# Attention stage of a YOCO decoder step: projections by token half in two accumulators, o by K half and token half, attention pieces between single K steps

## The reference

```python
def _shared_kv(x, pos, ln_kv, w_kv, k_norm):
    kv = _rms(x, ln_kv) @ w_kv
    ...
    k = _rope(_rms(k, k_norm), pos)
    return k, v

def _sink_attend(q, k, v, mask, sink):
    s = jnp.einsum('...qhgd,...khd->...hgqk', q.astype(jnp.float32), k.astype(jnp.float32)) * (HEAD_DIM ** -0.5)
    s = jnp.where(mask, s, NEG_INF)
    sk = sink.astype(jnp.float32)[:, :, None, None]
    m = jnp.maximum(jnp.max(s, axis=-1, keepdims=True), sk)
    p = jnp.exp(s - m)
    denom = jnp.sum(p, axis=-1, keepdims=True) + jnp.exp(sk - m)
    o = jnp.einsum('...hgqk,...khd->...qhgd', p / denom, v.astype(jnp.float32))

def _window_layer(x, pos, kk, vv, mask, ln, w_q, q_norm, sink, w_o, banded):
    q = (_rms(x, ln) @ w_q).reshape(B, L, N_HEADS, HEAD_DIM)
    q = _rope(_rms(q, q_norm), pos)
    ...
    return o.reshape(B, L, N_HEADS * HEAD_DIM) @ w_o
```

## Time and profile before

| what | value |
|---|---|
| median of three runs | 1665.57 us (1665.43 to 1666.39) |
| the profiled execution: its own time, its span | 1669.15 us, 1667.4 us |
| PE, PEld busy | 1586.8 us (95%), 1469.3 us (88%); 11246 instructions each |
| DVE, ACT, POOL busy | 841.2 us (50%), 510.7 us (31%), 145.3 us (9%) |
| share of the chain that ended last | PE 81%, DVE 9%, ACT 3%, DMA 3%, issue 2% |
| mean granted TensorE clock | 0.972 of full speed |

### The profile page before, as it was taken

The page is one execution under the profiler, slowest core; times in us unless marked ns, Lnnn a source line. Parts: engine busy times, 40 slices in busy tenths (PEclk is TensorE's granted clock), DMA queues, the critical chain, the costliest instruction groups (busy, mean ns, idle before and its releaser), DMA issues.

```text
span 1667.4 us, 27494 instructions
## 1 busy us (share of the span) xinstructions
PE 1586.8 (95%) x11246; PEld 1469.3 (88%) x11246; DVE 841.2 (50%) x1105; ACT 510.7 (31%) x778; POOL 145.3 (9%) x129
## 2 busy tenths in 40 slices
PE   7999999999999899999999999887789999999998
PEld 7688878968987799999999999865679999999997
DVE  6557438536734774434333485664546343443343
ACT  4243144224315332212222243244323221222221
POOL 0000001001000250000000040222132000000001
PEclk9999999999999999999999999885999999999999
DMA  6246217214423442222322232310012222222223
GB/s 229 82 156 212 86 57 253 90 65 167 154 73 104 139 144 87 89 88 77 99 88 89 76 101 86 99 43 14 26 39 78 100 87 91 76 101 77 97 79 104
DMA packets 51314, 166.80 MB, mean 100 GB/s; under 512 B 5920, under 2 KB 6256, under 8 KB 51200
## 3 DMA queue, kind: packets, MB, share of 16 engines
q1 hardware_dynamic: 43808, 137.35, 25.8%
q0 software_dynamic: 6704, 25.99, 4.3%
q10 hardware_dynamic: 720, 2.26, 0.3%
HBM read 141.36 MB, written 23.46 MB: 99 GB/s over the span
## 4 chain that ended last, share of the span: by engine, by line
PE 81%; DVE 9%; ACT 3%; DMA 3%; issue 2%; POOL 1%; DVEq 0%; SPq 0%; ACTq 0%; POOLq 0%
PE ps L422 63%; PE ps L436 8%; PE ps L948 2%; PE ps L942 2%; DVE arena L1384 2%; DVE w_lo L410 1%; PE ps L1192 1%; PE ps L930 1%; DVE x L1384 1%; DMA arena<-in_state 1%; DMA out_st_s<-arena 1%; PE ps L1171 1%; DVE arena L1724 1%; DMA w_raw<-in_w 1%; PE ps L1179 1%
## 5 line engine op out<-in xcount | busy, mean ns | idle before, releaser
L422 PE MATMUL ps<-xg_hi,w_hi 128*128 128x272 f32 x1728 | 363.9, 292 | 15.3 <-DVE xg_lo L1390 8.3
L422 PE MATMUL ps<-xg_hi,w_lo 128*128 128x272 f32 x1728 | 359.0, 289 | 0.0
L422 PE MATMUL ps<-xg_lo,w_hi 128*128 128x272 f32 x1728 | 358.0, 289 | 0.0
L405 ACT ACTIVATE w_hi<-w_raw 128x1024 fp32r<-128x1024 f32 x220 | 226.9, 1051 | 375.1 <-PE ps L422 213.3
L422 PE MATMUL ps<-pr_hi,w_hi 128*128 128x272 f32 x1440 | 307.5, 293 | 12.5 <-DVE pr_lo L1384 3.7
L410 DVE TENSOR_TENSOR w_lo<-w_raw,w_hi 128x1024 fp32r<-128x1024 f32 x220 | 279.3, 1287 | 64.2 <-ACT w_hi L405 59.1
L422 PE MATMUL ps<-pr_hi,w_lo 128*128 128x272 f32 x1440 | 304.3, 291 | 0.0
L422 PE MATMUL ps<-pr_lo,w_hi 128*128 128x272 f32 x1440 | 303.2, 291 | 0.0
L422 PEld LDWEIGHTS ps<-xg_hi,w_hi 128*128 128x128 f32 x1728 | 274.0, 189 | 30.6 <-issue 15.6
L422 PEld LDWEIGHTS ps<-xg_lo,w_hi 128*128 128x128 f32 x1728 | 273.1, 190 | 0.0
L422 PEld LDWEIGHTS ps<-xg_hi,w_lo 128*128 128x128 f32 x1728 | 271.6, 190 | 0.0
(11 more groups left out here) (207 smaller groups left out, 1298.5 us busy)
## 6 DMA issues: line engine op xcount, KB each, us to landing
w_raw<-in_w SPq DMA_DIRECT2D x220, 512.0 KB, 3.7
arena<-in_state SPq DMA_DIRECT2D x32, 512.0 KB, 4.6
out_st_s<-arena POOLq DMA_DIRECT2D x32, 512.0 KB, 4.3
arena<-arena SPq DMA_DIRECT2D x40, 68.0 KB, 2.1
x<-in_x ACTq DMA_DIRECT2D x4, 544.0 KB, 6.2
out_y<-x POOLq DMA_DIRECT2D x8, 272.0 KB, 2.3
out_st_p<-arena SPq DMA_DIRECT2D x4, 512.0 KB, 2.8
arena<-in_dec POOLq DMA_DIRECT2D x4, 256.0 KB, 2.9
```

What stands on the lines that cost most here:

```text
L405: nc.scalar.activation(w_hi[:, n.c % 4, :], w_raw[:, n.c % 2, :], ACT.Copy).then_inc(w_hi_done, 1)
L422: last = pe.matmul(ps[:, 2 * bank_pair + s, 0:HT], w_of(w, k), xm[:, k, s * HT:(s + 1) * HT], start=(k == 0 and w == 0 and xi == 0), stop= ...
```

## The change

The planned order of the stage is replaced on all five queues by one that is written out line by line. What it does:

- Every projection is computed for one token half at a time (`proj(i, s, a, z)`: output tile i, token half s, K steps a to z, three matmuls each). The halves take turns in two single banks, 0 and 1 (`U_BANK`). PE waits for the bank's last reader (`u_free`), which is ACT's square after DVE's copy for K and q, and DVE alone for V and o.
- o is cut by K half and token half, `out_part(x_, m, s, a, z)`: token half 0 of K half 0 needs only units 0, 1 and s0, token half 1 needs units 2 and 3; the same with units 4, 5, s1 and 6, 7 for K half 1. DVE adds each part to x by itself (`x_part`). The last eight parts have a bank each. The split for the second SwiGLU is made by token half (`next_hi`, `next_lo`).
- Pieces of attention stand between single K steps over the whole stage.
- All `keep_t` copies are on ACT. `scores_s` issues its matmuls with the two row halves in turn (r inside b) and no longer one half after the other. V is put between K and q, and its parts are copied one by one (`v_kept`).
- K is not scaled by the row's RMS factor before its own norm; an extra product with `eps64` brings the epsilon in (`head_sums` has four matmul calls, not two), so `stats_mm`'s two 272-column products and the 544-wide square root and reciprocal of this place go.
- The two cache writes of the sample tokens take one DMA each, not eight.

The core of the diff:

```diff
+U_ORDER = (*(("p", i, s) for i in range(2) for s in range(2)), *(("v", t) for t in range(5)), *(("p", i, s) for i in range(2, 10) for s in range(2)),
+           *(("o", x, m, s) for x in range(2) for s in range(2) for m in range(KT)))
+U_BANK, U_BEFORE, U_HALF = {}, {}, {}
+for name in U_ORDER:
+    own = name[0] == "o" and name[1] == 1 and name[3] == 1
+    U_BANK[name] = name[2] if own else len(U_BANK) % 2
...
+            def u_begin(name, n):
+
+                pe.wait_ge(w_lo_done, n + 1)
+                if U_BANK[name] < 2 and U_BEFORE[name]:
+                    pe.wait_ge(u_free[U_BANK[name]], U_BEFORE[name])
...
+            def steps(name, w_of, mov, n_k, a, z):
+
+                s = name[-1]
+                hi, lo = mov
+                for k in range(a, z):
+                    for w, xm in ((0, hi), (0, lo), (1, hi)):
+                        last = pe.matmul(u_bank(name), w_of(w, k), xm[:, k, token_half(s)], start=(k == 0 and w == 0 and xm is hi), stop=(k == n_k - 1 and w == 1))
+                if z == n_k:
+                    u_end(name, last)
...
+            def out_part(x_, m, s, a, z):
+
+                name, n = ("o", x_, m, s), n_out(x_, m)
+                if a == 0:
+                    u_begin(name, n)
+                    if m == 0:
+                        need = (("s0", 0, 1), (2, 3), ("s1", 4, 5), (6, 7))[2 * x_ + s]
+                        pe.wait_ge(att_lo, max(V_AT[v] for v in need) + 1)
...
                 for s in range(2):
-                    last = pe.matmul(ps[:, 4 + s, 0:HT], ones64, q_sqs(i)[:, s * HT:(s + 1) * HT], start=True, stop=True)
+                    pe.matmul(ps[:, 4 + s, 0:HT], ones64, nrm[:, i, token_half(s)], start=True, stop=False)
+                    last = pe.matmul(ps[:, 4 + s, 0:HT], eps64, sqsum[:, token_half(s)], start=False, stop=True)
...
                 for b in range(B):
-                    pe.matmul(old[:, :, TD * b:TD * b + TD], kct[half(r), u, b * P:b * P + P], qt[half(r), 4 * u:4 * u + 4, TD * b:TD * b + TD], start=True, stop=True)
...
+                    for r in range(2):
+                        pe.matmul(banks[r][:, 0:P].rearrange("p (j t) -> p j t", j=4)[:, :, TD * b:TD * b + TD], kct[half(r), u, b * P:b * P + P],
+                                  qt[half(r), 4 * u:4 * u + 4, TD * b:TD * b + TD], start=True, stop=True)
...
-                else:
-                    pe.wait_ge(xo_done, m)
-                product(pe, 0, o_tile(n, m), 4, (xg_hi[:, 0:4, :], xg_lo[:, 0:4, :]), lambda k: beside_o(m, k) if k else None)\
-                    .then_inc(blocks if m % 2 else o_half, 1)
-            pe.wait_ge(att_lo, len(V_ORDER))
...
+            proj(8, 1, 0, 2)
+            scores(4)
+            turned_s(0, 0)
+            proj(8, 1, 2, 6)
+            turned(0, 1, 1)
...
+            out_part(0, 0, 0, 0, 4)
+            out_part(0, 1, 0, 0, 4)
+            scores_s(1)
+            out_part(0, 2, 0, 0, 4)
+            values(2)
...
-                V.tensor_copy(pt_of(p // 4)[:, :, kk, 256 * h:256 * h + 256], t_bank(name).rearrange("p (r c) -> p r c", r=2)).then_inc(t_sem(name), 1)
...
+                last = tt(x[:, m, cols], x[:, m, cols], u_bank(name), ALU.add)
```

More of the change, by code:

```diff
@@ new lines, in _ @@
+            swap(0)
+            swap(1)
+            weights(Index(N_ATT + 10))
+            swap(2)
+            weights(Index(N_ATT + 11))
+            swap(3)
+            swap(4)
+            weights(Index(N_ATT + 12))
+            swap(5)
+            weights(Index(N_ATT + 13))
+            swap(6)
+            weights(Index(N_ATT + 14))
+            swap(7)
+            k_cache()
+            swap(8)
+            weights(Index(N_ATT + 15))
+            swap(9)
+            weights(Index(N_ATT + 16))
@@ new lines, in u_end @@
+            def u_end(name, last):
+                if U_HALF[name] is not None:
+                    last.then_inc(u_half, 1)
+                else:
+                    last.then_inc(blocks, 2 if name[0] == "v" else 1)
+            def steps(name, w_of, mov, n_k, a, z):
[6 more added lines that the diff above has]
+                    u_end(name, last)
@@ new lines, in v_rows @@
+            def v_rows(t, a, z):
+                name = ("v", t)
+                if a == 0:
+                    pe.wait_ge(w_lo_done, N_ATT + 4)
+                    u_begin(name, N_ATT + 3)
+                for k in range(a, z):
+                    sl, at = (2, 3)[k // 4], (k % 4) * 256
+                    for i, (xm, w) in enumerate(((xg_hi, w_hi), (xg_lo, w_hi), (xg_hi, w_lo))):
+                        last = pe.matmul(ps[:, U_BANK[name], 0:256], xm[:, k, tok(t)], w[:, sl, at:at + 256], start=(k == 0 and i == 0), stop=(k == KT - 1 and i == 2))
+                if z == KT:
+                    u_end(name, last)
@@ L1139, in q_square_sums @@
                 bank = ring(("qs", j))
-                pe.wait_ge(q_sq, j + 1)
+                for s in range(2):
+                    pe.wait_ge(u_free[U_BANK["p", 2 + j, s]], U_BEFORE["p", 2 + j, s] + 1)
                 for c in range(NCH):
@@ L1299, in _ @@
+            proj(8, 1, 6, 8)
+            scores_back(0, 1)
+            scores(5)
+            values(0)
+            q_square_sums(4)
+            q_square_sums(5)
+            turned(1, 0, 0)
+            scores(6)
+            proj(9, 0, 0, 5)
+            turned(1, 0, 1)
+            turned(1, 1, 0)
+            turned(1, 1, 1)
+            proj(9, 0, 5, 8)
+            proj(9, 1, 0, 3)
+            turned_s(0, 1)
+            proj(9, 1, 3, 6)
             values(1)
-            scores(6)
@@ new lines, in _ @@
+            out_part(0, 6, 1, 0, 1)
+            turned(6, 0, 0)
+            turned(6, 0, 1)
+            out_part(0, 6, 1, 1, 3)
+            scores(15)
+            out_part(0, 6, 1, 3, 4)
+            values_s(1)
+            out_part(0, 7, 1, 0, 4)
+            turned(6, 1, 0)
+            turned(6, 1, 1)
+            out_part(1, 0, 0, 0, 4)
+            out_part(1, 1, 0, 0, 4)
+            out_part(1, 2, 0, 0, 4)
+            values(6)
+            turned(7, 0, 0)
+            turned(7, 0, 1)
@@ new lines, in _ @@
+            x_part(0, 3, 0)
+            maxima(10)
+            denominators(9)
+            maxima_s(1, 0)
+            x_part(0, 4, 0)
+            x_part(0, 5, 0)
+            maxima(11)
+            denominators(10)
+            probs_s(1, 0)
+            x_part(0, 6, 0)
+            out_lo(3)
+            x_part(0, 7, 0)
+            denominators(11)
+            maxima(12)
+            x_part(0, 0, 1)
+            x_part(0, 1, 1)
+            maxima_s(1, 1)
+            denominators(12)
```

1054 lines of the change are left out of this document (614 added, 440 removed), and 8 rows, old and new, of the table T_ORDER.

## The result

The changed kernel takes **1598.04 us** (median of 4 runs, 1596.96 to 1599.55) where the kernel before takes 1665.98 (4 runs, 1665.43 to 1672.0): a ratio of **0.9585**, 95% interval 0.9561 to 0.9609, faster. The prediction was 1606, with a range of 1590 to 1634. The profiled execution took 1598.72 us.

What follows compares the result with a forecast made beforehand. PE was taken to bound the kernel, with time to give only in the attention stage: 210 work + 7 clock + 6 idle = 223 us against 283, 60 us less, giving 1606 us. Range 1590 to 1634.

Steps and rivals of the forecast that it cites:

- The forecast case: Whole kernel: the change works as predicted, measuring 1594 to 1620 us, likeliest 1606; chance 0.68.
- PE's work: First K product to the SwiGLU third block's norm sums: 210 us at full clock after the change (206 to 215).
- The base of 211: Same stretch before the change: 283.0 less 44.8 idle and 27.0 lost to the clock leaves 211 us PE work.
- changes of form: PE switching between kinds of matmul in the stretch: about 20 more switches at 0.1 us, +2 us.
- The sample scores: scores_s, 64 instructions now alternating row halves: -4 us, total cost between 2.2 and 7.8 us.
- Idle: PE's waits in the stretch: 44.8 us before, 6 us after, with 2 and 20 as bounds.
- the cover that the prediction counted on: Bank hand-overs: the other half's matmuls hide the readers, 3.0 us for q and 1.5 us for o.
- Clock: PE's clock in the stretch: four falls to 1.2 GHz, costing 7 us (3 to 14).
- The rival of a clock that stays low: Stretch from 1022 on: clock low for 40% of some 165 us, 41 us more, measuring 1640; chance 0.08.
- DVE near 155: DVE's busy time in the stretch: near 155 us, against 160.9 before.
- The rival that DVE paces the halves: Bank hand-overs: each of 52 halves waits 2 us for DVE, idle 104 us, measuring 1704; chance 0.04.
- The late order: Rope or softmax pieces held by a late neighbour on DVE, ACT or POOL: 35 us idle, measuring 1635; chance 0.13.

Runs made afterwards that it cites:

- q ahead of the units: Changed kernel with the last five and seven eighths q halves and their sums run before the sample scores and all units: 1617.40 us.
- o in one accumulator: Changed kernel with the halves of o in one accumulator instead of two, K, V and q keeping both: 1618.59 us.
- o by K half only: Changed kernel with the first K half of o's eight parts for the first token half moved behind the values of unit 3: 1607.98 us.
- scores not alternated: Changed kernel with the 64 sample scores ordered all of one row half, then all of the other: 1604.63 us.
- ends and sums: Changed kernel with POOL's squares summed by token half, the first K half's last step later, and few-column q sums pulled apart: 1599.02 us.
- half ends: Changed kernel with every attention piece inside a half of a product, from the q projection on, moved to that half's nearer end: 1597.14 us.

## Why the prediction was right

The forecast case came true, 8 us below the forecast and inside the range. By its steps:

- **PE's work: 210 forecast (206 to 215), 205 found.** Of the 208.6 us busy, the rows above lose 3.6 to the clock (each row's busy time by one less its clock). The base of 211 was about 0.5 too high: cut into stretches of 3 us instead of six large ones, the kernel before loses 27.7 to the clock and 44.9 to idle of its 283.0, which leaves 210.5. With the head_sums at +1.8, the norm sums at -0.9 and the scores at -3.9 this makes 207.5, over 2 us more than was found, and the changes of form, forecast at +2, would add to that. That term had the wrong sign: counted in the two traces, PE goes over between projection steps and other forms 76 times in the stretch, against 110 before. Stops count as well. A matmul of 272 columns lasts 0.29 us in the rows and the next one starts 0.125 after it, so by estimate a stop adds about 0.16 us of busy time, and there are 4 stops instead of 25. What each of the two is worth was not measured.
- **The sample scores: -4 forecast, with 0 and -5.6 as bounds, -3.9 found.** Sixteen take half of 1.96 us, under the 1.3 that was named. The alternation alone gives 2.7; the other 1.2 is against the earlier trace rows, where a run of sixteen took 0.12 each and not the 0.10 of the unalternated run here. The Trainium skill (TensorE: Matmul & The Clock Gate, "The mechanism" of its part on row and column tiling) has a weight load overlap a running matmul only where the row group differs. The runs agree in the direction; the bound of -5.6, which the prediction put beside it, is not reached.
- **Idle: 6 forecast, 4.6 found**, and where it was named: POOL's squares (0 to 2 forecast, 2.35 found; a tile takes POOL 1.53 + 1.53 us instead of the 1.09 + 1.71 of the earlier trace rows) and the last feature tile ahead of K (parts of a microsecond forecast, 1.4 found). No transpose waits for POOL, and one half of 49 that take over a bank waits for its reader, 0.6 us: the cover that the prediction counted on is missing at the one place where two halves in a row have the same bank (it counted 52 hand-overs; 49 halves wait for a reader in the program). What the experiments add is that this rests on all of these parts: without the second accumulator for o, 14.8 us of idle come back, without the q projection beside the units 11.2, without o's token halves 4.5.
- **Clock: 7 forecast (four falls), 3.4 to 3.6 found (two falls of 1.7).** The size of one fall and the pieces it follows were right, the number was not. The rival of a clock that stays low is refuted for this order; it is the state of PE with the pieces and their waits alone, 0.50 over 20 us with q ahead of the units. Taking the banks in turn did not bring it: the clock of the stretch is 0.98 with two accumulators, where PE stops at one hand-over, and 0.98 with one for o, where it stops at 13 for 0.62 to 2.51 us and has one fall more. The Trainium skill (same page, "A second HAM failure mode: psum-queue depth-cycling") tells of a kernel whose cycling through banks let PE stop briefly between groups of matmuls, so that its clock swung. The run with one accumulator, which has such stops, shows no more than that one fall; with two there are hardly any stops, so these runs don't test it.
- **DVE near 155: 159.0 found**; the halves take 0.43 (x) and 0.49 (q), but its SBUF operations average 1.11 us against 0.95 in the earlier trace rows. ACT, forecast at 115, has 111.2. The rival that DVE paces the halves fell with the waits above, and 14 copies more on DVE add no wait of a half.

```profile
L1625 DVE TENSOR_TENSOR arena<-arena 128x544 f32<-128x544 f32 x22 | 24.4, 1109 | 4.2 <-DMA arena<-arena 2.5 <-POOL arena L594 1.3 <-DVE q_fac L1625 0.2
...
L1625 DVE TENSOR_TENSOR x<-x,ps 128x272 f32<-128x272 f32 x32 | 13.7, 430 | 10.6 <-PE ps L1283 10.6
...
L1894 DVE TENSOR_SCALAR arena<-ps,gain 128x272 f32<-128x272 f32 x20 | 9.9, 494 | 4.9 <-PE ps L1283 4.7
```

```profile
L551 POOL TENSOR_TENSOR sq<-x 128x544 f32<-128x544 f32 x7 | 10.7, 1530 | 1.7 <-DVE x L1625 1.2
L554 POOL TENSOR_TENSOR sqsum<-sqsum,sq 128x544 f32<-128x544 f32 x7 | 10.7, 1525 | 0.6
```

- **The sum: 223 forecast, 213.2 found**; 60 us less forecast, 69.8 found: 40.2 of idle, some 24 of clock, the rest work. All three terms came out below their forecast, so the time lies near the prediction's low ends (211, 1594 us). The late order (35 us of idle) did not happen; the order has spare time, since pieces moved by up to 1.5 us changed idle by 1.2 us. Of the 69.8 us, single edits give back 22 (q ahead of the units), 19 (o in one accumulator), 10 (o by K half only) and 7 (scores). No run takes back all of them at once, and V's place, K without its RMS factor and the cache writes were not taken back, so how the whole divides among the parts is not shown.

What stays open: why a fall of the clock lasts 3.4 us in one kernel and 10 in another behind the same pieces (scores not alternated, ends and sums), why one kernel with the same run of sums has none (half ends), and how far this changes from one execution to the next.

## What to carry to other kernels

Cut the large products so finely that work with no open inputs can stand beside every chain of small steps, and count that work twice: it takes the chain's waits, and it keeps PE's clock up, which in the run with q ahead of the units was worth as much. A second accumulator pays when the reader and its hand-overs (0.6 us here) have nothing else beside them; the finer choice, at which step of a half a piece stands, was worth nothing. Before a small piece is moved, ask what it covers: the sums that seemed to cost a fall of the clock were also the cover of a hand-over. And look for two parts in a row in the same bank: the one such place of this order was the one hand-over that PE waited at.

## What the runs showed of the hardware

- PE without any idle time fell to 1.2 GHz after runs of small forms, and PE with 16% of idle in small forms alone stayed there for 20 us; two executions of one program had the two falls at the same places, while a third, 4 us faster, had a higher mean clock (0.995 against 0.992).
- Few-column matmuls (16 columns, 64 rows) take 0.06 us each with alternating row halves and 0.10 in runs of sixteen of one half.
- Handing a bank from PE to DVE's 0.44 us addition and back leaves PE idle for 0.62 us where nothing else stands between.
- SBUF operations of the same size took different times in the two kernels: POOL's square of a 544-wide tile 1.53 us on average against 1.09 in the earlier trace rows, its sum 1.53 against 1.71, DVE's 544-wide additions and products 1.11 against 0.95. Whether POOL and DVE slow each other was not tested.
